# Attention in pairs of heads, with the projections laid between them in pieces of 128 columns

## The reference

```python
h = _rmsnorm(x, g_mix)
u = h @ w_in
fq = u[..., OFF_FQ:OFF_FK].reshape(b, t, FOX_HEADS, FOX_HD)
...
dv = u[..., OFF_DV:IN_COLS].reshape(b, t, DIFF_HEADS, 2 * DIFF_HD)
...
s = (jnp.einsum('bqhd,bkhd->bhqk', qblk, k).astype(jnp.float32) * scale
     + jnp.transpose(cq, (0, 2, 1))[..., None] - c_k_t)
s = jnp.where(k_pos[None, :] <= qp[:, None], s, NEG_INF)
p = jax.nn.softmax(s, axis=-1)
return jnp.einsum('bhqk,bkhd->bqhd', p.astype(v.dtype), v)
...
a = jax.nn.softmax(s, axis=-1)
w = a[:, :, 0] - lam * a[:, :, 1]
return jnp.einsum('bhqk,bkhe->bqhe', w.astype(v.dtype), v)
...
x = x + mixed @ w_o
x = x + _moe(_rmsnorm(x, g_ffn), w_r, b_r, w_gate, b_gate, w_up, b_up, w_down, b_down)
```

## Time and profile before

| | us |
|---|---|
| median of 3 runs | 1416.14 |
| lowest and highest | 1415.52, 1420.9 |
| the profiled execution | 1417.97 |
| its span in the profile | 1416.2 |
| PE busy | 1339.8 (95%) |
| DVE busy | 293.9 (21%) |
| ACT busy | 179.7 (13%) |
| start of the transposition of the attention's rows | 254.36 |

### The profile page before, as it was taken

One profiled execution on the slowest core, in us unless ns is written; L12 is line 12 of the kernel. 1 busy time (PEld: TensorE's weight loads), 2 busy tenths in 40 slices (PEclk: granted clock), 3 DMA queues, 4 the chain that ended last, 5 costly groups with the idle time before them and its releaser, 6 DMA issues.

```text
span 1416.2 us, 15874 instructions
## 1 busy us (share of the span) xinstructions
PE 1339.8 (95%) x6091; PEld 520.8 (37%) x6091; DVE 293.9 (21%) x844; ACT 179.7 (13%) x414; POOL 74.1 (5%) x143
## 2 busy tenths in 40 slices
PE   5999979978999999999999999999999999999967
PEld 4646446442333333333333333333333333333332
DVE  2014375032111111111111111111111111111152
ACT  2013233100100010000100001000010000000132
POOL 5000011000000000000000000000000000000000
PEclk9999985787999999999999999999999999999989
DMA  9701232445999999999999999999999999999631
GB/s 333 273 1 60 85 123 84 189 179 212 412 427 429 427 430 427 427 429 429 429 427 430 429 429 428 428 428 429 429 428 428 429 427 429 428 428 428 246 132 37
DMA packets 52274, 478.07 MB, mean 338 GB/s; under 512 B 8824, under 2 KB 9440, under 8 KB 25820
## 3 DMA queue, kind: packets, MB, share of 16 engines
q1 hardware_dynamic: 46264, 464.29, 78.6%
q0 software_dynamic: 3920, 13.13, 2.6%
q10 hardware_dynamic: 2068, 0.37, 0.2%
HBM read 468.54 MB, written 14.47 MB: 341 GB/s over the span
## 4 chain that ended last, share of the span: by engine, by line
PE 57%; DMA 38%; DVE 3%; ACT 1%; issue 1%; POOL 0%; ACTq 0%; POOLq 0%; SPq 0%
PE ps L682 52%; DMA ring<-in_w_up 37%; PE ps L920 1%; PE ps L694 1%; DMA ring<-expert_rows 1%; DMA X<-in_x_sample 0%; PE ps L787 0%; DVE ring L1101 0%; DVE X L1319 0%; DVE mx L1113 0%; ACT ring L599 0%; PE ps L789 0%; DMA expert_rows<-area,rowi 0%; PE ps L993 0%; PE ps L815 0%
## 5 line engine op out<-in xcount | busy, mean ns | idle before, releaser
L682 PE MATMUL ps<-ring,area 128*64 128x512 f32 x3264 | 729.6, 597 | 13.4 <-DMA ring<-in_w_up 13.4
L682 PEld LDWEIGHTS ps<-ring,area 128*64 128x64 f32 x3264 | 224.0, 137 | 489.3 <-issue 437.2
L682 PE MATMUL ps<-area 32*64 32x512 f32 (+2 forms) x960 | 170.2, 410 | 0.8 <-ACT ring L566 0.7
L1265 DVE TENSOR_SCALAR area<-ps 128x512 f32<-128x512 f32 x34 | 23.5, 692 | 452.8 <-PE ps L682 452.8
L682 PE MATMUL ps<-H,area 128*64 128x512 f32 (+1 forms) x420 | 105.7, 621 | 3.4 <-DVE area L1241 3.4
L682 PEld LDWEIGHTS ps<-area 32*64 32x64 f32 (+2 forms) x960 | 55.4, 140 | 124.5 <-issue 121.6
L496 POOL DMA_INDIRECT expert_rows<-area,rowi x34 | 33.1, 974 | 998.7 <-ACT area L636 998.7
L682 PE MATMUL ps<-ring,hT 128*128 128x512 f32 (+1 forms) x192 | 79.0, 606 | 0.5 <-ACT hT L611 0.5
L682 PE MATMUL ps<-hT,ring 128*128 128x320 f32 x256 | 73.5, 447 | 0.0
L625 ACT ACTIVATE area<-ps 128x512 f32<-128x512 f32 x35 | 20.9, 597 | 409.3 <-PE ps L682 409.3
L1269 DVE TENSOR_SCALAR area<-ps 128x512 f32<-128x512 f32 x34 | 23.5, 692 | 219.9 <-PE ps L682 219.9
(11 more groups left out here) (184 smaller groups left out, 567.7 us busy)
## 6 DMA issues: line engine op xcount, KB each, us to landing
ring<-in_w_gate SPq DMA_DIRECT2D x68, 2048.0 KB, 23.0
ring<-in_w_up SPq DMA_DIRECT2D x68, 2048.0 KB, 25.4
ring<-in_w_down SPq DMA_DIRECT2D x68, 2048.0 KB, 21.4
ring<-in_w_in SPq DMA_DIRECT2D x6, 2048.0 KB, 16.9
ring<-in_w_o SPq DMA_DIRECT2D x2, 2048.0 KB, 7.7
early<-in_w_ple_gate SPq DMA_DIRECT2D x1, 4096.0 KB, 23.3
ring<-expert_rows POOLq DMA_DIRECT2D x2, 2048.0 KB, 10.6
ring<-running_logs SPq DMA_DIRECT2D x8, 416.0 KB, 3.4
```

Source lines behind the costliest of these rows:

```text
L682: return T.matmul(out, lhsT, rhs, start=first, stop=last)
L1265: V.tensor_scalar(gate, ps[:, G_BANK, :], LIMIT, None, ALU.min).then_inc(g_sb, 1)
```

## The change

Attention works in 8 pairs of units that share a matrix slot (`PAIRS`); `scores(p)` issues both, each matmul of the lower row group followed by the one of the upper, into four PSUM banks. The products are reordered (`PRODUCTS`), two before attention, twenty beside pairs 0 to 6 (`FILL`); late products all use bank 7. q and k columns are loaded as 16 chunks of 128 columns into 8 slots; the v columns as a whole. The v product of the sample tile is split into two halves of 256 columns on the two column groups. The new keys' rows are transposed at the end. The relative bias's DMAs move to GpSimd's queue, w_o's loads behind the fox logs, and the squares and scaling of the diff heads to pairs 5 and 6. ScalarE's order follows.

```diff
+CHUNK_SLOTS = 8
...
+        squares_of = ring[:, 2, 3072:4096].rearrange("p (t n) -> p t n", t=2)
+        chunks = ring[:, 3:5, :].rearrange("p b n -> p (b n)")
+        wv = piece(0)
+        wout = [piece(3), piece(4)]
...
-        PRE_SLOT = [0, 1, 2, 3, 4, 0, 3, 4]
         OFF_D = OFF_FF + FH
-        PRE_COL = [OFF_D, OFF_D + GW, OFF_D + 2 * GW, 0, GW, 2 * GW]
-        GROUPS = [4, 8, 11, 15, 19, 22]
-        PRODUCTS = [(pc, m) for pc, kind in enumerate("qkvqkv") for m in range(3 if kind == "v" else 4)]
-        FILL = [1, 1, 2, 1, 2, 1, 2, 1]
-        FILLED = [GROUPS[2] + sum(FILL[:u]) for u in range(len(FILL) + 1)]
+        OFF = {(1, "q"): OFF_D, (1, "k"): OFF_D + GW, (1, "v"): OFF_D + 2 * GW, (0, "q"): 0, (0, "k"): GW, (0, "v"): 2 * GW}
+        PRODUCTS = [(1, "q", 0), (1, "k", 0),
+                    (1, "q", 1), (1, "k", 1), (1, "v", 0), (1, "v", 1), (1, "v", 2),
+                    (1, "q", 2), (1, "k", 2),
+                    (1, "q", 3), (1, "k", 3), (0, "v", 0),
+                    (0, "q", 0), (0, "k", 0), (0, "v", 1),
+                    (0, "v", 2), (0, "q", 1), (0, "k", 1),
+                    (0, "q", 2), (0, "k", 2),
+                    (0, "q", 3), (0, "k", 3)]
+        BEFORE, EARLY = 2, 7
+        FILL = [5, 2, 3, 3, 3, 2, 2, 0, 0]
+        FILLED = [BEFORE + sum(FILL[:p]) for p in range(len(FILL) + 1)]
         assert FILLED[-1] == len(PRODUCTS)
+        CHUNKS = [i for i, (x, kind, m) in enumerate(PRODUCTS) if kind != "v"]
         def product_bank(i):
-            return i % 6 if i < GROUPS[2] else 2 + i % 2
+            return (4, 7, 4, 7, 5, 6, 4)[i] if i < EARLY else 7
...
+        def out_bank(i):
+            return 6 + (i % 2 if i >= 8 else 0)
         def score_bank(u):
-            return 2 * (u % 2) if u >= len(FILL) else 0
+            return 2 * (u % 2)
...
+        PAIRS = NU // 2
+        def outs_of(p):
+            return [i for i, us in enumerate(OUTS) if 0 <= p < PAIRS and us[0] // 2 == p]
...
-            for i in range(5):
-                load_pre(i)
...
+            def load_chunk(k):
+                x, kind, m = PRODUCTS[CHUNKS[k]]
+                o = OFF[x, kind] + m * P
+                sp.dma_start(chunk(k), w_in[:, :, o:o + P]).then_inc(wqk[k % CHUNK_SLOTS], 16)
+            def load_values(x):
+                sp.dma_start(wv, w_in[:, :, OFF[x, "v"]:OFF[x, "v"] + GW]).then_inc(wv_in, 16)
+            for k in range(4):
+                load_chunk(k)
+            load_values(1)
+            for k in range(4, CHUNK_SLOTS):
+                load_chunk(k)
             for x, n in enumerate(("cache_fox_v", "cache_diff_v")):
                 sp.dma_start(vcache[x], A[n].rearrange(RE[n], p=P)).then_inc(vc_in, 16)
-            sp.wait_ge(relvec, 1)
-            sp.dma_start(rvec[:, :], bvec).then_inc(rel_out, 16)
...
-            sp.dma_start(relb, skew).then_inc(rel_in, 16)
-            for i in range(5, 8):
-                sp.wait_ge(u_ps, GROUPS[(0, 3, 4)[i - 5]])
-                load_pre(i)
...
+            def load_logs(h):
+                if h >= 2:
+                    sp.wait_ge(s_sb, 2 * DH + h - 1)
+                sp.dma_start(logs[:, h % 2, :], cscr[h:h + 1, :].to_broadcast([P, KEYS])).then_inc(logs_in[h % 2], 16)
             sp.wait_ge(ct_sb, 1)
             sp.dma_start(cscr[:, :], CT).then_inc(logs_out, 16)
             sp.wait_ge(logs_out, 16)
...
+            load_logs(0)
+            load_logs(1)
+            sp.wait_ge(u_ps, EARLY)
+            load_values(0)
+            for k in range(CHUNK_SLOTS, len(CHUNKS)):
+                sp.wait_ge(u_ps, CHUNKS[k - CHUNK_SLOTS] + 1)
+                load_chunk(k)
+            for h in range(2, FH):
+                load_logs(h)
+            sp.wait_ge(u_ps, len(PRODUCTS))
+            for h in range(2):
+                sp.dma_start(wout[h], w_o[:, :, h * GW:(h + 1) * GW]).then_inc(wout_in, 16)
...
+            link(last)
+            g.dma_start(rvec[:, :], bvec).then_inc(rel_out, 16)
+            pool.wait_ge(rel_out, 16)
+            g.dma_start(rscr.rearrange("h p n -> p h n")[:, :, 0:768], rvec.unsqueeze(0).to_broadcast([P, DH, 768])).then_inc(rel_rows, 16)
...
+            g.dma_start(relb, skew).then_inc(rel_in, 16)
...
-            pool.wait_ge(u_ps, GROUPS[2])
+            for t in range(NT):
+                r = ROWS[t]
+                power(ssd[0:r, t, :], DH, 1.0 / P, SUB_EPS, sub_ss, t + 1, sub_rstd)
...
+                elif m < 2:
+                    ins = s.activation(vnew[x][:, m, :], ps[:, b, :], ACT.Copy)
                 else:
-                    ins = s.activation(vnew[x][0:ROWS[m], m, :], ps[0:ROWS[m], b, :], ACT.Copy)
+                    for n in range(2):
+                        ins = s.activation(vnew[x][0:DEC, m, n * 256:(n + 1) * 256], down(ps[:, b, 0:256], n), ACT.Copy)
...
+            def exponents(u):
...
+            for p in range(PAIRS + 1):
+                fills = iter(range(FILLED[p], FILLED[p + 1]))
+                outs = outs_of(p - 1)
+                for i in itertools.islice(fills, 1):
+                    evac_product(i)
+                if p < PAIRS:
+                    exponents(2 * p)
+                if not outs:
+                    exponents(1)
+                for j, o in enumerate(outs):
+                    evac_PT(o)
+                    if j == 0 and p < PAIRS:
+                        exponents(2 * p + 1)
+                    for i in itertools.islice(fills, 1):
                         evac_product(i)
+                    evac_O(o)
+                for i in fills:
+                    evac_product(i)
...
+                x, kind, m = PRODUCTS[i]
+                b = product_bank(i)
+                if kind == "v":
+                    pe.wait_ge(wv_in, 16 * (2 - x))
                 else:
...
+                    k = CHUNKS.index(i)
+                    pe.wait_ge(wqk[k % CHUNK_SLOTS], 16 * (k // CHUNK_SLOTS + 1))
+                if bank_before(i) is not None:
+                    pe.wait_ge(u_sb, bank_before(i) + 1)
+                elif b in (5, 6):
+                    pe.wait_ge(ct_sb, 1)
                 for c in range(DC):
...
+                    if kind != "v":
+                        last = mm(ps[:, b, 0:NTOK], chunk(k)[:, c, :], hT[:, c, :], c == 0, c == DC - 1)
+                    elif m < 2:
+                        last = mm(ps[:, b, :], hT[:, c, COL[m]:COL[m] + P], wv[:, c, :], c == 0, c == DC - 1)
                     else:
...
+                        for n in range(2):
+                            last = mm(down(ps[:, b, 0:256], n), hT[:, c, 0:DEC], wv[:, c, n * 256:(n + 1) * 256], c == 0, c == DC - 1)
                 last.then_inc(u_ps, 1)
...
-            for i in range(GROUPS[2]):
+            pe.wait_ge(kc_sb, 8)
+            for i in range(BEFORE):
                 project(i)
-                if i + 1 == GROUPS[0]:
-                    cumsums()
...
+            def scores(p):
+                x, m, hb = UNITS[2 * p]
+                pe.wait_ge(u_sb, PRODUCTS.index((x, "k", m)) + 1)
+                if p > 0:
+                    pe.wait_ge(s_sb, 2 * p)
...
+                    for hb in range(2):
+                        pb, o = 64 * hb, 512 * score_bank(hb)
+                        last = mm(psf[0:r, o + a0:o + a1], qT[x][pb:pb + HD, m, COL[t]:COL[t] + r], kT[x][pb:pb + HD, m, k0:k0 + a1 - a0], True, True)
+                        if n == len(parts) - 1:
+                            last.then_inc(s_ps, 1)
...
-                    pe.wait_ge(o_sb, i - 1)
-                b = 6 + i % 2
+                b = out_bank(i)
+                if i == 9:
+                    pe.wait_ge(u_sb, len(PRODUCTS))
+                elif i > 0:
+                    pe.wait_ge(o_sb, i - 1 if i > 9 else i)
...
+                pe.wait_ge(s_sb, NU)
                 for g8 in range(8):
                     x, m = g8 // 4, g8 % 4
-                    if g8 >= 2:
-                        pe.wait_ge(kr_sb, 2 * (g8 - 1))
+                    if g8 >= 4:
+                        pe.wait_ge(kr_sb, 2 * (g8 - 3))
...
-            pe.wait_ge(u_sb, GROUPS[1])
-            for u in range(NU + 3):
-                if u < NU:
-                    if u == len(FILL):
-                        pe.wait_ge(u_sb, len(PRODUCTS))
-                    if u == len(FILL) + 1:
-                        pe.wait_ge(kr_sb, 16)
-                    scores(u)
-                if u == 2:
-                    pe.wait_ge(u_sb, GROUPS[2])
+            for p in range(PAIRS + 1):
+                if p < PAIRS:
+                    scores(p)
+                if p == 1:
+                    pe.wait_ge(u_sb, EARLY)
                     pe.wait_ge(ct_sb, 1)
                     pe.wait_ge(vc_in, 32)
-                if u == len(FILL):
+                fills = iter(range(FILLED[p], FILLED[p + 1]))
+                for i in itertools.islice(fills, 1):
+                    project(i)
+                for o in outs_of(p - 1):
+                    transpose_probs(o)
```

(29 more changed lines are left out.)

## The result

The changed kernel takes 1382.59 us in the median of 4 runs (1380.91 to 1384.91) against 1418.12 us for the kernel before in the same comparison, a ratio of 0.9746 with a 95% interval of 0.9725 to 0.9767: 35.5 us less. Its profiled execution took 1380.91 us, the fastest of the four, with a span of 1379.1 us.

A forecast was written before the change was run, and what follows sets the result against it. PE's own work bounds up to 175.64 us, then a chain of waits; rebuilding PE's queue (49.0, plus 137.9 for pairs, 2.2 scores, 33 tail) ends attention at 222.1 instead of 254.36 us: 1384 us, range 1374 to 1402.

The forecast's parts named there:

- the stretch without products: Old kernel, 175.64 to 254.36 us: PE busy 64.37 of 78.72 us at clock 0.67, bound by waits around PE, DVE, ACT.
- from their end to the transposition of the rows: Tail after the last pair's scores, without products: 33 us, from 189.1 to 222.1 us, mostly at low clock.
- the rest of the span: Everything after attention, experts included: order as before, so 254.36 to 1416.2 us carried over unchanged.
- The two unshown prices: Costs absent from the trace: a pair's alternating scores, taken as 2.2 us, and the split v product, 3.6 us.
- S: PE time for one pair's scores on two row groups: taken as 2.2 us, between 1.96 (whole overlap) and 3.92 (none).
- the factor of 0.51 from the column pairs: Experts' alternating 64-column matmuls: 0.224 us against 0.436 at whole width, used to price a pair's scores.
- The step on the other engines' cover: Pairs 0 to 6: DVE and ACT work hidden under PE; weights ready at 9.9 us, next scores 11.9 or more behind.
- the two waits for ScalarE: Pairs 5 and 6: PE waits for ACT's evacuation of transposed weights, 0.8 + 0.3 us, making 15.2 us each before scores.
- a warm tail: Rival: full clock throughout the tail, 27 us instead of 33, giving 1378 us; chance 0.08.
- row groups that don't overlap: Rival: in scores, each of eight pairs costs 1.7 us more, giving 1398 us; chance 0.15.
- Bank 7: Rival: 15 late products each wait 0.6 us for ACT's evacuation, PE loses 9 us, giving 1393 us; chance 0.10.
- Chunks: Rival: w_in loads with 512 B rows, 11.9 us each, arrive late, giving 1424 us; slower from about 11.4; chance 0.03.

The follow-up runs named there:

- e1: Changed kernel with a pair's scores issued one head after the other instead of alternating between row groups: 1403.57 us, ratio 0.9893 to the kernel before.
- e2: Changed kernel with the v product of the 64 sample rows in one piece of 512 columns again: 1388.88 us.
- e3: Changed kernel with the four products of pairs 5 and 6 moved to pairs 1 to 4: 1399.58 us, ratio 0.9871 to the kernel before.
- e6: Changed kernel with one product behind each of the two transpositions in pairs 5 and 6, ScalarE's order following: 1375.98 us.
- e4: Changed kernel with ScalarE evacuating the last pair's transposed weights ahead of the exponentials of unit 14: 1376.08 us.
- e8: Changed kernel with each w_in chunk loaded as four strips of 32 columns, 4096 rows of 128 B instead of 1024 of 512 B: 1381.27 us.
- e5: Changed kernel with ten extra matmuls of 320 columns, results unread, nine in TensorE's tail gap and one before values 9: 1376.98 us.

## Why the prediction was right, point by point

The forecast was 1384 us, measured were 1382.6. That the two lie within 1.4 us is in part luck. The span was forecast as 1384.0 and was 1379.1 us, 4.9 less. The forecast took the profiled execution to lie 1.8 us above the median, as it had before; after the change it lay 1.7 below it, which hides 3.5 of the 4.9 us. The gain, forecast as 32.2 us, was 35.5.

The mechanism held: PE's queue, rebuilt with the new costs, gave the time. Each part was undone alone. The row groups (e1) cost 21.0 us, of which 13.7 are the overlap; the halves (e2) cost 6.3 us; four of the seven products beside fox pairs (e3) cost 17.0 us. These prices don't add up to the gain: each is what the part is worth with the others in place, and in e1 and e3 part of it is the clock.

Where the 36 us came from is better read from the two long windows of the table above. Idle time gave 2.9 us of them. PE's busy time fell by 33.5 us: at full clock 15.6 for the row groups (eight pairs, 1.95 us each) and 6.8 for the two split v products. The other 11, an estimate by difference that no run separates, fit the clock, 0.91 on the mean instead of 0.87. The prediction read the stretch without products as a chain of waits. That was so for its 14.35 idle us, but in the window at low clock of the earlier trace rows PE was busy for 4.00 of 4.00 us: there its own work at half the clock was the bound. With products beside them the pairs ran at a mean clock of 0.97, against 0.67 for the stretch without products before; of waits the change still has 11.5 us, 9.1 of them in the tail.

By steps:

| step | forecast us | measured us |
|---|---|---|
| start of the first pair's scores | 49.0 | 47.8 |
| scores of a pair, at full clock | 2.2 | 1.97 |
| split v product | 3.6 | 3.6 |
| pair 0 | 28.5 | 28.1 |
| pairs 1, 2, 3 | 14.1, 21.1, 21.1 | 13.8, 20.9, 20.9 |
| pair 4, with the wait for the k | 18.3 (wait 0.6) | 18.2 (wait 0.53) |
| pairs 5 and 6 | 17.4 each | 17.8, 19.5 |
| scores of the last pair begin | 186.9 | 186.9 |
| from their end to the transposition of the rows | 33 | 28.2 |
| the rest of the span | 1161.8 | 1161.0 |

The two unshown prices went to their favourable bound or to the value taken: S came out at 1.97 us, which is whole overlap, so the factor of 0.51 from the column pairs was the right row to lean on and the allowance above it was not needed. The step on the other engines' cover held: no product waited for DVE or for bank 7 (the wait of 0.53 us is the scores' for the k just made, priced at 0.6), and squares and scaling ended at 163.7 and 184.1 us, ahead of the next scores.

That the last pair's scores began at the forecast 186.9 us was in part luck. The terms that were mis-sized cancel: the beginning was 1.2 us shorter, pairs 0 to 4 were 1.2 us shorter together, and pairs 5 and 6 were 2.5 us longer, because the prediction kept the clock at full up to the last scores. It priced the two waits for ScalarE (1.1 us, measured 0.95) and not what comes behind them: scores of 3.70 us, values of 2.6 and 2.2 us (1.6 at full clock) and a product of 4.84 us instead of 4.41. e6 removed both waits and with them 5.7 us.

In the tail the forecast took the low clock for the whole of it. It held for values 8 and 9 (2.9 us each against 3.0), then the clock came back during the new keys' rows: these took 5.0 us instead of 6.5 and the last two outputs 7.6 instead of 11. Those two make up the 4.8 us by which the tail was shorter. The chance of 0.08 stood for a warm tail; it was half warm.

The tail's gap of 5.4 us was in the sum (values 8 at +6.4 us, measured +6.4), but the prediction took it as given by VectorE's first unit. e4 shows that 4.45 us of it came from ScalarE's order.

The rivals: row groups that don't overlap are what e1 makes by order, and then a pair costs the forecast 3.92 us; the rival's 14 us of that price would have been 13.7 us, plus what the clock adds. Bank 7 didn't bind in this order of the products, but its price was the forecast one: e3 shows it, 0.62 us wherever two products follow each other. Chunks are far from their threshold, by e8. The Trainium skill (TensorEngine Tiling (Array Packing), Key Properties) says that a change of tiling mode drains the engine; here its cost is small at most: a product of 8 matmuls takes 4.41 us between scores and transposition in the changed kernel, and 4.51 us between two units' scores in the kernel before (104.44 to 108.95), against 4.37 us in the mean of four in the earlier trace rows. The Trainium skill (DMA: Bandwidth & Descriptors) gives 512 B as the least transfer for line rate. The trace differs: from 84 to 92 us, with chunk loads alone in the queue, the rate was 291 GB/s at a full DMA share, against the 388 GB/s of the earlier trace rows for rows of 2048 B, so a chunk cost 1.8 us instead of 1.4. It changed nothing here, as e8 shows.

## What to carry to other kernels

Where a chain over three engines has no work under it, lay independent matmuls under each of its links, and count how long the bare chain takes: that is the cover to be filled. But split the gain into idle time and busy time before naming its cause: here PE waited hardly less than before, and did less and did it faster. A short wait of TensorE is not priced by its length when the matmuls around it are small: look at the clock of the rows behind it, and in more than one trace. And before a gap is put down to the engine that was last, read what the releasing engine had in its queue ahead of the release; another order of ScalarE's work in the last pair was worth 4.5 us of a gap of 5.4.

## What the runs showed of the hardware that I had not expected

Two 64-row matmuls in float32 on different row groups overlap wholly when they alternate in the queue (1.97 us for 16 instructions, 1.96 us for 8 of one group alone), and not at all when the order is one group's eight and then the other's (3.92 us). The granted clock fell behind waits of 0.95 us amid values and transpositions (from 165 us in the changed kernel), with PE waiting for nothing else since 149.65 us. It did not do so every time: behind the second such wait it fell in the changed kernel (scores of 2.96 us) and stayed at 1.00 in e4 and e5 (1.97 us), with the same instructions up to there. Behind the empty gap of 5.4 us values 8 ran at the low clock, with the scores ahead of it at full clock (e6); with nine matmuls in the gap they ran at 1.00 (e5). Loads with rows of 128, 512 and 2048 B ran at 163, 291 and 388 GB/s. And the same beginning reached its first scores between 47.8 and 51.7 us in different traces, by the clock between 28 and 40 us, which is as much as several of the effects studied here; lengths between two marks of a trace told them apart better than positions.
